# Where the last sixteen top-k rounds run in a fused two-block kernel: two per step over eight attention steps, or one per step over sixteen

## What is computed

```python
topk = min(TOPK_MAX, S // 4)                 # 128
dots = einsum('bqhd,bsd->bqhs', qi, k_idx)
score = einsum('bqhs,bqh->bqs', relu(dots), wi)
score = where(key_pos[None, :] <= t[:, None], score, -inf)
_, idx = lax.top_k(score, topk)
...
s = where(valid, s, NEG_INF)                 # attention over the chosen keys
p = softmax(s)
```

## Time and profile before

| what | value |
|---|---|
| median of 3 runs | 2265.41 us |
| lowest and highest | 2264.39 and 2265.88 us |
| the profiled execution | 2267.34 us |
| span of its records | 2265.6 us |
| mean granted clock of TensorE in it | 0.952 of full speed |
| PE busy | 2045.6 us, 90% of the span |
| DVE busy | 1259.7 us, 56% |
| ACT busy | 685.0 us, 30% |
| POOL busy | 735.3 us, 32% |

### The profile page before, as it was taken

How to read it: one execution, slowest core, us unless ns; L and a number is a source line. 1 busy time by engine, 2 the same in 40 slices (tenths; PEclk the granted TensorE clock), 3 DMA queues, 4 the chain that set the end, 5 groups by cost and what they waited for, 6 DMA issues and landing times.

```text
span 2265.6 us, 25526 instructions
## 1 busy us (share of the span) xinstructions
PE 2045.6 (90%) x9608; PEld 1609.5 (71%) x9608; DVE 1259.7 (56%) x2106; ACT 685.0 (30%) x1097; POOL 735.3 (32%) x181
## 2 busy tenths in 40 slices
PE   6898789899899977898999999778998888999996
PEld 4775567688778865566888888557886766888885
DVE  5869975634943877766446434563333466322336
ACT  4223462321122125452221221223443323212221
POOL 2431103344443431114344443221320423444442
PEclk8998999999999988899999999789999999999998
DMA  4221002322532520003325322212210221223221
GB/s 171 93 75 56 24 12 68 139 104 90 204 113 94 192 95 31 24 24 109 112 91 185 124 87 90 84 56 75 75 57 20 74 75 62 100 77 113 104 77 63
DMA packets 31484, 199.12 MB, mean 88 GB/s; under 512 B 3488, under 2 KB 3616, under 8 KB 13344
## 3 DMA queue, kind: packets, MB, share of 16 engines
q1 hardware_dynamic: 26496, 164.64, 21.2%
q10 hardware_dynamic: 4896, 33.25, 3.9%
HBM read 195.78 MB, written 2.10 MB: 87 GB/s over the span
## 4 chain that ended last, share of the span: by engine, by line
PE 49%; DVE 5%; ACT 1%; issue 1%; POOL 0%; ACTq 0%; DVEq 0%
PE psum L1315 42%; PE psum L1337 1%; PE psum L1481 1%; DVE work L921 1%; DVE work L900 1%; PE psum L1446 1%; PE psum L1463 1%; PE psum L1418 1%; PE psum L1710 1%; DVE h_lo L904 1%; DVE xT L916 0%; DVE work L910 0%; DVE work L925 0%; POOL w_lo L533 0%; DVE xT L910 0%
## 5 line engine op out<-in xcount | busy, mean ns | idle before, releaser
L533 POOL TENSOR_TENSOR w_lo<-raw,w_hi 128x2048 fp32r<-128x2048 f32 (+2 forms) x176 | 734.9, 4176 | 1499.1 <-ACT w_hi L550 1499.1
L1315 PE MATMUL psum<-h_hi,w_hi 128*128 128x512 f32 x1560 | 620.0, 397 | 23.6 <-POOL w_lo L533 12.1
L1315 PE MATMUL psum<-h_lo,w_hi 128*128 128x512 f32 x1560 | 616.4, 395 | 0.0
L1315 PE MATMUL psum<-h_hi,w_lo 128*128 128x512 f32 x1560 | 616.0, 395 | 0.0
L550 ACT ACTIVATE w_hi<-raw 128x2048 fp32r<-128x2048 f32 (+2 forms) x176 | 301.2, 1712 | 594.8 <-PE psum L1315 487.0
L1315 PEld LDWEIGHTS psum<-h_hi,w_hi 128*128 128x128 f32 x1560 | 296.9, 190 | 101.6 <-issue 19.7
L1315 PEld LDWEIGHTS psum<-h_hi,w_lo 128*128 128x128 f32 x1560 | 296.9, 190 | 64.7 <-issue 2.4
L1315 PEld LDWEIGHTS psum<-h_lo,w_hi 128*128 128x128 f32 x1560 | 296.9, 190 | 62.6 <-issue 2.2
L1315 PE MATMUL psum<-g_hi,w_hi 128*128 128x512 f32 x528 | 206.7, 391 | 8.1 <-issue 5.0
L1315 PE MATMUL psum<-g_hi,w_lo 128*128 128x512 f32 x528 | 205.6, 389 | 0.0
L1315 PE MATMUL psum<-g_lo,w_hi 128*128 128x512 f32 x528 | 205.6, 389 | 0.0
(11 more groups left out here) (259 smaller groups left out, 2514.7 us busy)
## 6 DMA issues: line engine op xcount, KB each, us to landing
raw<-w_up SPq DMA_DIRECT2D x66, 1024.0 KB, 4.9
raw<-w_dn SPq DMA_DIRECT2D x48, 704.0 KB, 4.0
mod_w<-w_mod ACTq DMA_DIRECT2D x24, 1024.0 KB, 5.7
raw<-w_c_in SPq DMA_DIRECT2D x13, 1024.0 KB, 4.9
raw<-w_a_in SPq DMA_DIRECT2D x11, 1024.0 KB, 4.8
raw<-w_b_in SPq DMA_DIRECT2D x7, 1024.0 KB, 4.9
raw<-w_a_out SPq DMA_DIRECT2D x8, 640.0 KB, 3.8
raw<-w_b_out SPq DMA_DIRECT2D x8, 640.0 KB, 3.9
```

The lines of the kernel that those rows point to most:

```text
L533: nc.gpsimd.tensor_tensor(LO[slot][:, 0:ph.size], RAW[slot][:, 0:ph.size], HI[slot][:, 0:ph.size].bitcast(F32), ALU.subtract).then_inc(lo_ ...
L1315: ins = nc.tensor.matmul(out, l, r, start=(k == 0 and m == 0), stop=(k == n - 1 and m == 2))
```

## The change

DVE runs one round in each of its turns 0 to 15, where it ran two in each of its turns 0 to 7. The closing `tensor_scalar` moves from turn 7 to turn 15. Number, size and order of the rounds are the same, and so is everything on the other engines.

```diff
--- before.py
+++ after.py
@@ -1201,9 +1201,8 @@
                     norm("ckv", None, None, dst=(CH, CL), parts="low")
 
             def a_between(k):
-                if k < 8:
-                    pick_eight(ROWT - 1, False)
-                    pick_eight(ROWT - 1, k == 7)
+                if k < 16:
+                    pick_eight(ROWT - 1, k == 15)
             attend(a_all, a_between)
 
             def derive():
```

## The result

The changed kernel takes 2275.71 us (median of 5 runs, 2274.55 to 2277.32), the kernel before 2265.41 us (5 runs, 2264.26 to 2265.88). The ratio is 1.0047, with a 95% interval of 1.0032 to 1.0062: 10.3 us slower, 0.45%. Later, in another group of runs (e11), the ratio was 1.0045 (1.0031 to 1.0059).

What follows compares the result with a forecast made beforehand. The prediction took PE to carry the kernel, with DVE's rounds hidden in the memory steps but not from turn 9 on. Terms 0 + 9.4 + 0.8 = +10.2 us on 2265.41 gave 2275.6 us, range 2273.6 to 2279.0.

Steps and rivals of the forecast that it cites:

- The memory steps hide the rounds: Turns 0 to 7: taking eight rounds out only lengthens DVE's wait, from some 0.9 to 2.4 us; effect 0.
- The circle PE, ACT, PE: Memory steps: PE's transposes, ACT's copies and bank emptying, PE's products and scores repeat every 5.46 us, without DVE.
- Turn 8 free, turn 9 dear: Turn 8's round fits the 1.62 us wait before turn 9; turn 9's round delays turn 10 by 1.52 us.
- Turns 10 to 15: DVE never idle, turns 10 to 12 taking 2.40 us each; turn 16 starts 9.4 us late, turn 9's delay included.
- the prediction's own sign of being wrong: Stated condition for the forecast to be wrong: turns 10 to 15 of DVE less than 2.3 us apart.
- Nothing won back later: From turn 16 on, the delay stays in full; bounds of 0 and 0.5 us saved, nothing taken back.
- The clock: PE at 1.2 GHz in turns 10 to 15 for free, then a 3.8 us stretch after turn 16 costing 0.8 us.
- The upper rival: Clock stays low well into the 256-key turns: 9.4 + 3.8 = 13.2 us, so 2278.6 us; chance 0.15.
- The rival of the clock gate: PE works in every changed turn, so the clock stays full, clock term 0: 2274.8 us; chance 0.17.
- Not slower: DVE bounds the memory steps: 12.6 us off the front against 9.4 us added behind, 2262.2 us; chance 0.02.

Runs made afterwards that it cites:

- e11: The changed kernel unaltered, timed again in a later group of runs: 2275.08 us, ratio 1.0045 to the kernel before.
- e1: Kernel before with one round in each of turns 0 to 7 and none after, the other eight left out: 2265.84 us, ratio 1.0001.
- e2: Kernel before with its two rounds in turns 0 to 7 kept and one more added in each of turns 8 to 15: 2276.88 us, ratio 1.0047.
- e5: Kernel before, but ACT empties the two filled banks of a memory step before copying the transposes: 2263.68 us, ratio 0.9982.
- e8: Kernel before with two rounds in turns 0 to 6, one in turn 7, one plus the closing instruction in turn 8: 2267.89 us, ratio 1.0001.
- e9: Changed kernel with unread products of constants in PE's waits at steps 8 to 16, only 256 columns at step 8: 2275.50 us, ratio 1.0037.
- e10: Kernel before with ACT emptying the banks first, plus unread PE products of constants at steps 8 and 9: 2259.07 us, ratio 0.9967.
- e4: Kernel before with unread PE products of constants at steps 8 (512 columns) and 9 only: 2265.48 us, ratio 1.0001.
- e3: Changed kernel with unread PE products of constants at steps 8 to 15, 512 columns at step 8: 2276.19 us, ratio 1.0047.

## Why the prediction was right, point by point

The forecast was 2275.6 us and the result is 2275.7. The mechanism was right in all its main steps, but so close a hit is luck: two terms were off in opposite directions, by 0.56 and 1.4 us, and what they leave went under in the scatter between executions.

- **The memory steps hide the rounds: right, and shown.** The trace has 5.42 us a step and 2.35 us of waiting, the prediction said 5.46 and 2.4. e1 took the rounds out with no effect and e2 left them in with none. The circle PE, ACT, PE was named from rows; e5 broke it at the link that was named, and the steps became 4.76 us.
- **Turn 8 free, turn 9 dear: right.** Turn 10 came 1.5 us later, the prediction said 1.52 (300.55 for 299.03). e8 shows the free one alone.
- **Turns 10 to 15: right in kind, 0.56 us too much in size.** They took 15.02 us in place of 7.68, so 7.34 more, the prediction had 7.9 (9.42 less the 1.52 of turn 9). The step that was off is the 2.40 us of a turn. I took a turn's own work from the first start to the end of L994 (0.88 us), but the round's first instruction starts 0.79 us after L973 (299.36 to 300.15), ahead of the recorded end of L994. Distances between starts would have been the right measure, as for the round itself (1.51), and as the section on the profile before says. 2.30 us a turn is what was measured, just at the prediction's own sign of being wrong ("less than 2.3 us apart").
- **Nothing won back later: right.** From turn 24 to the projection both kernels take 36.29 us (102.35 - 66.06 and 113.23 - 76.94).
- **The clock: right in kind, much too small in size.** The forecast had 0.8 us, measured were 2.2 us in turns 16 to 24 (e9). That the clock costs nothing in turns 10 to 15 was right (15.02 us at either level). The stretch at 1.2 GHz after turn 16 was taken as 3.8 us from a row of before, and it was 7.6; the clock was back at about 322, not 321. The upper rival had priced just that length, at 3.8 us with no cover, of which 2.2 came: 1.6 us was covered; that the waits which PE has there in any case did it, as the 1.16 us that I had read from the earlier trace rows would suggest, is not shown. It isn't a fixed amount: in e2 the same place cost 0.7, in e11 2.1 us, by where the clock was when turn 16 began and when it came back.
- **The rival of the clock gate.** Ahead of the fall PE's longest waits were 1.07 and 0.83 us. In all turns at 1.2 GHz PE did something, and the longest wait ahead of a matmul in 299 to 316 was 1.21 us; all the same the clock stayed at 0.50 throughout. In e11 it did come back during turn 15, and fell again in a wait of 1.98 us. The Trainium skill (TensorE: Matmul & The Clock Gate, "HAM oscillation") ties the fall to gaps of idle PE longer than any that occurred here; the measurement decides against it, for this pattern of short matmuls between short waits. What rule the clock follows here stays open.
- **Not slower: out.** e1 gives what the removal of rounds is worth where they were: 2265.84 against 2265.44 us. Only in turns 0 and 1, for which the prediction quoted no row, was DVE without slack, and that gave 0.15 us.

The sum by measured terms is 1.5 + 7.3 + 2.2 = 11.0 us for turns 8 to 24 (11.1 unrounded), where the forecast had 10.2. The medians differ by 10.3 and the ratio's interval goes from 7 to 14 us; the profiled pair had 0.9 us less after the projection had started, 0.2 less from turn 0 to turn 8 and 1.0 less ahead of turn 0, which makes its 9.0 us of span. The 0.15 us of turns 0 and 1 are part of the 0.2; I did not look for a cause of the others.

## What to carry to other kernels

What an instruction off the critical path costs is read turn by turn, from the wait that stands behind it: here two rounds in a turn that waits were free, one behind which no wait stood cost its full length (1.5 us in turn 9), one behind which small waits stood cost the rest (1.1 to 1.2 us in turns 10 to 12), and an even spread took work out of the first kind of turn and put it into the others. Before spreading, look whether the place that is to be relieved has a wait for that engine at all; here it had none, and a link of another engine (in which order ACT empties banks) set the pace. When an engine newly becomes the bound, ask what its delay does to TensorE's clock, also in the stretch behind it.

## What was not expected

- The fall of the clock cost most where DVE no longer was the bound. Keeping PE busy with products that nobody reads held it at 1.00 and was worth 2.2 us in e9 and 1.9 us in e10. The products have to fit into the wait: at step 8, where the 512 columns stood ahead of the scores, they cost 0.4 us of the 0.6 that they gained (e4).
- One wait left open was enough. In e3 PE had extra products in steps 8 to 15 and the clock still fell in the one wait of 1.98 us ahead of step 16, and nearly all of the gain was gone (14.02 us in turns 16 to 24 against 14.21 without products and 11.96 in e9).
- The kernel before had 6.0 us to give in the same stretch, 4.0 of them by exchanging two entries in the order of ACT: from turn 0 to the projection it took 102.35 us, e5 98.31 and e10 96.37.
